# Three adaptive-modulation sums of a transformer kernel, started and reduced at other places

## The reference

```python
mod = (jax.nn.silu(c) @ w_ada[l] + b_ada[l]).reshape(b, N_SUB, 3, D_MODEL)

def sublayer(h, i, fn, resid_w):
    shift, scale, gate = mod[:, i, 0, None, :], mod[:, i, 1, None, :], mod[:, i, 2, None, :]
    u = rms_norm(h, norm_pre[l, i]) * (1.0 + scale) + shift
    return h + resid_w * gate * rms_norm(fn(u), norm_post[l, i])
```

## Time and profile before

| | us |
|---|---|
| median of 3 runs (lowest, highest) | 1827.97 (1821.05, 1828.79) |
| the profiled execution's own time | 1828.06 |
| its span | 1826.4 |
| PE busy | 1713.1 (94%) |
| DVE busy | 992.3 (54%) |
| ACT busy | 821.5 (45%) |
| POOL busy | 581.0 (32%) |

### The profile page before, as it was taken

The page is one execution under the profiler, slowest core; times in us unless marked ns, Lnnn a source line. Parts: engine busy times, 40 slices in busy tenths (PEclk is TensorE's granted clock), DMA queues, the critical chain, the costliest instruction groups (busy, mean ns, idle before and its releaser), DMA issues.

```text
span 1826.4 us, 21892 instructions
## 1 busy us (share of the span) xinstructions
PE 1713.1 (94%) x7939; PEld 1421.0 (78%) x7939; DVE 992.3 (54%) x984; ACT 821.5 (45%) x966; POOL 581.0 (32%) x378
## 2 busy tenths in 40 slices
PE   6999999999999999979879999999997987789998
PEld 5888779878888888768767888788886875678886
DVE  4445668575655565643466645654456433565444
ACT  6565541454445344424344444544445455554343
POOL 0000000188885888852888900000000010500000
PEclk9999999999999999979878999999998997789999
DMA  6656453267784778645334765546563521425552
GB/s 215 204 186 212 147 192 110 91 218 243 243 263 147 255 238 260 228 157 189 93 117 159 231 197 185 178 147 193 186 214 119 208 92 47 138 92 185 186 185 88
DMA packets 208278, 321.35 MB, mean 176 GB/s; under 512 B 10920, under 2 KB 146402, under 8 KB 208226
## 3 DMA queue, kind: packets, MB, share of 16 engines
q1 hardware_dynamic: 195968, 281.05, 47.0%
q0 software_dynamic: 10512, 38.54, 6.8%
q10 hardware_dynamic: 1746, 1.05, 0.2%
HBM read 319.55 MB, written 1.05 MB: 176 GB/s over the span
## 4 chain that ended last, share of the span: by engine, by line
PE 74%; POOL 9%; DVE 7%; ACT 5%; issue 4%; DMA 1%; ACTq 0%; POOLq 0%; SPq 0%; DVEq 0%
PE ps L544 21%; PE ps L546 21%; PE ps L545 21%; POOL arena L508 3%; POOL arena L505 3%; DVE w_lo L1606 2%; POOL arena L510 2%; PE ps L590 1%; PE ps L842 1%; ACT w_hi L1181 1%; PE ps L780 1%; PE ps L648 1%; POOL arena L512 1%; PE ps L597 1%; PE ps L947 1%
## 5 line engine op out<-in xcount | busy, mean ns | idle before, releaser
L1606 DVE TENSOR_TENSOR w_lo<-raw,w_hi 128x2048 fp32r<-128x2048 f32 x256 | 630.7, 2472 | 326.1 <-ACT w_hi L1181 325.9
L544 PE MATMUL ps<-w_hi,actT_hi 128*128 128x512 f32 x1504 | 605.6, 403 | 21.1 <-DVE actT_lo L1634 7.8
L546 PE MATMUL ps<-w_hi,actT_lo 128*128 128x512 f32 x1504 | 594.5, 395 | 0.0
L545 PE MATMUL ps<-w_lo,actT_hi 128*128 128x512 f32 x1504 | 594.4, 395 | 0.0
L1181 ACT CAST w_hi<-raw 128x2048 fp32r<-128x2048 f32 x266 | 506.1, 1911 | 192.1 <-PE ps L546 190.4
L544 PEld LDWEIGHTS ps<-w_hi,actT_hi 128*128 128x128 f32 x1504 | 288.3, 192 | 82.5 <-DVE actT_lo L1634 8.5
L546 PEld LDWEIGHTS ps<-w_hi,actT_lo 128*128 128x128 f32 x1504 | 287.5, 191 | 62.5
L545 PEld LDWEIGHTS ps<-w_lo,actT_hi 128*128 128x128 f32 x1504 | 288.5, 192 | 57.7
L544 PE MATMUL ps<-w_hi,hT_hi 128*128 128x512 f32 x480 | 188.1, 392 | 2.6 <-DVE hT_lo L1731 2.6
L545 PE MATMUL ps<-w_lo,hT_hi 128*128 128x512 f32 x480 | 187.5, 391 | 0.0
L546 PE MATMUL ps<-w_hi,hT_lo 128*128 128x512 f32 x480 | 187.5, 391 | 0.0
(11 more groups left out here) (255 smaller groups left out, 1455.4 us busy)
## 6 DMA issues: line engine op xcount, KB each, us to landing
raw<-ffn_w_in_dram SPq DMA_DIRECT2D x176, 512.0 KB, 4.8
raw<-ffn_w_out_dram SPq DMA_DIRECT2D x88, 512.0 KB, 4.4
arena<-w_ada_dram POOLq DMA_DIRECT2D x72, 512.0 KB, 5.0
raw<-ffn_w_gate_dram SPq DMA_DIRECT2D x44, 512.0 KB, 3.9
raw<-ffn_w_up_dram SPq DMA_DIRECT2D x44, 512.0 KB, 4.9
raw<-ffn_w_down_dram SPq DMA_DIRECT2D x44, 512.0 KB, 4.5
raw<-w_in_dram SPq DMA_DIRECT2D x40, 512.0 KB, 4.5
raw<-hg_w_in_dram SPq DMA_DIRECT2D x32, 512.0 KB, 4.6
```

Source lines behind the costliest of these rows:

```text
L544: nc.tensor.matmul(to, hi, whi, start=start, stop=False, skip_group_check=True)
L545: nc.tensor.matmul(to, hi, wlo, start=False, stop=False, skip_group_check=True)
L546: return nc.tensor.matmul(to, lo, whi, start=False, stop=stop, skip_group_check=True)
L1606: nc.vector.tensor_tensor(w_lo[:, s, :], raw[:, s, :], w_hi[:, s, :].bitcast(F32), ALU.subtract)\
```

## The change

POOL begins with piece 0 as soon as `silu(c)` is there, inside the first feed-forward stage, and does the `levels` copy and the zeroing behind it. Pieces 1 and 2 follow one another without a wait between them, since piece 2 is summed into a region of its own. PE reduces piece 0 behind the second chunk of hg_in, and pieces 1 and 2 between the feed-forward stage of norm 2 or 3 and the stage behind it, after the transposes of that stage's first tile. DVE's `modulation` follows in hg_in, norm 3 and norm 4. POOL's last splits of fox_in stand behind piece 2.

```diff
 HG_ORDER = (1, 0, 2, 3)
+ADA_AT = {1: 0, 3: 1, 4: 2}
...
-        ada_acc = region(12288, ADA_W)
+        ada_acc = [region(at, ADA_W) for at in (12288, 12288, 8192)]
...
-        levels_raw = region(14336, LEVEL_AT[-1])
+        levels_raw = region(10240, LEVEL_AT[-1])
...
-            pool.wait_ge(levels_loaded, 16)
-            pool.wait_ge(hT_turned, NF + 1)
-            nc.gpsimd.tensor_copy(levels, levels_raw).then_inc(levels_ready, 1)
-            pool.wait_ge(levels_ready, 1)
-            nc.gpsimd.memset(hg_sc_flat, 0.0).then_inc(hg_zeroed, 1)
-
-            pool.wait_ge(turned, 4 * (by_name["hg_out"].turned + 1))
-            pool.wait_ge(c_ready, 1)
...
-            for piece in range(3):
-                if piece:
-
-                    pool.wait_ge(ada_reduced, piece)
+            def ada_piece(piece):
                 for s in range(2):
                     ada_load(piece, s, s)
-                if piece == 2:
-                    split_gate_weights(by_name["fox_in"])
...
+            pool.wait_ge(c_ready, 1)
+            ada_piece(0)
+            pool.wait_ge(levels_loaded, 16)
+            pool.wait_ge(hT_turned, NF + 1)
+            nc.gpsimd.tensor_copy(levels, levels_raw).then_inc(levels_ready, 1)
+            pool.wait_ge(ada_reduced, 1)
+            nc.gpsimd.memset(hg_sc_flat, 0.0).then_inc(hg_zeroed, 1)
+            pool.wait_ge(turned, 4 * (by_name["hg_out"].turned + 1))
+            ada_piece(1)
+            ada_piece(2)
+            split_gate_weights(by_name["fox_in"])
             pool.wait_ge(ada_reduced, 3)
...
-                if st.norm in (3, 4, 6):
-                    ada_reduce({3: 0, 4: 1, 6: 2}[st.norm])
+                if st.norm == 1:
+                    ada_reduce(ADA_AT[st.norm])
...
                 turn_next(st, 0)
+                nxt = following[id(st)]
+                if nxt is not None and nxt.norm in (3, 4):
+                    ada_reduce(ADA_AT[nxt.norm])
...
                 chunk(st, 0, 1)
+                after_second_chunk(st)
                 chunk(st, 1, 0)
                 pe.wait_ge(kept0, st.kept + 2)
                 pe.wait_ge(kept1, st.kept + 2)
+                pe.wait_ge(mod_ready, 1)
                 turn(hg_z, 0)
...
-                pe.wait_ge(mod_ready, 2)
+                pe.wait_ge(mod_ready, 3)
...
                 weights(4)
+                act.wait_ge(levels_ready, 1)
...
                 keep(1)
+                modulation(st)
                 weights(3)
```

More of the change, by code:

```diff
@@ L511, in ada_unit @@
                 pool.wait_ge(ada_by2, n + 1)
-                nc.gpsimd.tensor_tensor(ada_acc[:, bass.ds(u * ADA_U, ADA_U)], r[:, 0, :], r[:, 1, :], ALU.add)\
+                nc.gpsimd.tensor_tensor(ada_acc[piece][:, bass.ds(u * ADA_U, ADA_U)], r[:, 0, :], r[:, 1, :], ALU.add)\
                     .then_inc(ada_summed, 1)
                 pool.wait_ge(ada_summed, n + 1)
-            for piece in range(3):
-                if piece:
-                    pool.wait_ge(ada_reduced, piece)
+            def ada_piece(piece):
                 for s in range(2):
                     ada_load(piece, s, s)
-                if piece == 2:
-                    split_gate_weights(by_name["fox_in"])
                 with pool.Fori(0, ADA_N // 2 - 1) as i:
@@ L774, in ada_reduce @@
             def ada_reduce(piece):
+                if piece == 0:
+                    pe.wait_ge(consts_loaded, 16)
                 pe.wait_ge(ada_summed, ADA_N * (piece + 1))
@@ L779, in ada_reduce @@
                 for u in range(ADA_N):
-                    last = nc.tensor.matmul(ps[:, SMALL_BANK, u:u + 1], ada_acc[:, u * P:(u + 1) * P],
+                    last = nc.tensor.matmul(ps[:, SMALL_BANK, u:u + 1], ada_acc[piece][:, u * P:(u + 1) * P],
                                             C["ones"][:, 0:1], start=True, stop=True)
@@ L1654, in modulation @@
                 n = st.norm
-                if n in (3, 4, 6):
-                    piece = {3: 0, 4: 1, 6: 2}[n]
+                if n in ADA_AT:
+                    piece = ADA_AT[n]
                     dve.wait_ge(ada_reduced, piece + 1)
```

## The result

The kernel after the change takes 1849.43 us (median of 4 runs, 1846.21 to 1850.34). The kernel before, run beside it, takes 1824.51 us (median of 4, 1818.99 to 1828.79). The ratio is 1.012, with a 95% interval of 1.0094 to 1.0145: slower, and by more than the 0.5% that a measurement of this kernel can tell. The two profiled executions have spans of 1847.7 and 1826.4 us, so the traces have 21.3 us to explain.

What follows compares the result with a forecast made beforehand. PE is busy 94%; POOL's chain counts only where PE waits for it. Terms 24.6 + 6.2 - 8.5 - 6 = +16.3 us on 1828.06 gave 1844.4 us, range 1832 to 1856.

Steps and rivals of the forecast that it cites:

- The inner range of 1836 to 1852: Whole kernel: the forecast case's time, given piece 0's end, low-clock losses, piece 2's end and the fox stage.
- Part A: Piece 0 in the first stages: PE waits for POOL in hg_in, third chunk effectively later by 24.6 us.
- I take 249: First stages: POOL's piece 0 ends at 249, nearer to the old piece 0's duration; bounds 246 to 253.
- the clock's 2.0: Behind hg_in's reduction: the low clock costs 2.0 us, between 1.4 and 2.3 in two earlier cases.
- The cover in the first stage: First stage and turn to hg_in: PE's some 9 us wait covers whatever piece 0 costs DVE and PE.
- The first rival: hg_in: piece 0 done before PE arrives, no wait, A falls to 8.5 us, time 1828 to 1831; chance 0.14.
- Part B: Pieces 1 and 2 reduced between the stages, norm 3 to fox_in: PE waits for POOL twice, +6.2 us.
- Part C: Norm 6: the reduction is taken out and gives back its price without a wait, -8.5 us.
- Part D: Fox stage: without POOL's piece 2 alongside, stretched DVE operations shorten, -6 us; bounds -12 to -2.7.
- The second: First stages: piece 0 slower than any measured, 9.6 us a unit, ending at 265, time 1860; chance 0.10.
- The third: Fox stage gives back 14 us, as DVE delays pass through exchanges between three engines; time 1836; chance 0.05.
- The fourth: The three reduction places: something other than POOL held PE, so the change might not act; no chance of its own given.

Runs made afterwards that it cites:

- the kernel with the reductions behind the chunks: Kernel after, with pieces 1 and 2 reduced behind the second chunks of norm 3 and fox_in, piece 0 still early: 1832.26 us, ratio 1.0014.
- the version with its own region: Kernel before, with only piece 1 summed into a region of its own, nothing else moved: 1817.66 us, ratio 0.9945; again 1817.15 us, ratio 0.9931.
- The third experiment: Kernel after, piece 0 reduced one chunk later in hg_in, pieces 1 and 2 behind the second chunks of norm 3 and norm 4: 1824.76 us, ratio 0.9978.

## Why the prediction was right, point by point

The predicted time was 1844.4, the measured 1849.4, and 1849.4 is within the range of 1832 to 1856. The side was right, and so was the mechanism: POOL's chain, not PE's, sets the end of three stretches. Against the profiled execution the sum was +16.3 and the traces have +21.3. The terms were off by +2.9, -1.4, +0.6, 0, +6.5 and -3.6, in the order of the table; that they sum to no more than 5.0 is in part luck. The inner range of 1836 to 1852 was narrower than its own bounds, which give 1831 to 1856 when they all fall on one side. Term by term:

**Part A, predicted +24.6, measured +27.5.** Piece 0 ended at 250.93, where I had taken 249 with bounds of 246 to 253: its 216.1 us are those of the old piece 0 (216.2), where I had drawn the value in a little for quicker last units. POOL started at 34.9, and its first unit was late, ending 17 us behind the start, since the first product waited for its load until 41.68 and then ran stretched. The later units were quicker, so the whole came out even. PE arrived at 241.0 and waited 10.1 us, not at 240 for 9. The reduction took 10.4 as predicted. The clock behind it stayed low for longer than assumed, at 0.55 in the mean for 6.7 us, and cost 2.9 us in place of 2.0: the third chunk took 13.8 us, where 48 products at 0.227 us each take 10.9. These rows are the reduction and the stretch behind it:

```profile
251.00:261.00 10.00, 9.92 (x47) 9.95 (x47) 0.00 (x0) 0.00 (x0) 0.66 (x1) 0.50 0.01 2
261.30:268.00 6.70, 6.70 (x18) 5.28 (x19) 4.92 (x5) 0.00 (x0) 1.80 (x1) 0.55 0.39 122
```

The steps that were short are "I take 249", by 1.9 us and inside its bounds, and the clock's 2.0, which came out above its upper bound of 2.3. The HGRN2 stage took 1.4 us less, which I had put at nothing, and in these two profiles only: the stretch varies by 3 to 5 us within each kernel, as shown above.

**The cover in the first stage** held. DVE's splits in norm 0 went from 2292 ns to this:

```profile
L1612 DVE TENSOR_TENSOR w_lo<-raw,w_hi 128x2048 fp32r<-128x2048 f32 x30 | 83.4, 2779 | 49.1 <-ACT w_hi L1186 49.1
```

2779 ns is what they take in norm 2 beside POOL, 2796. The feed-forward stage was no longer for it, +0.3 us. But the turn to hg_in was: PE's first product of hg_in waited 4.42 us for the rounded activations (2.03 before), and DVE's operation that scales them ahead of the transposes, 0.75 us before, took 3.05:

```profile
215.03 0.79 PE L542 MATMUL ps<-w_hi,actT_hi 128*128 128x512 f32 x1 [4.42 <-DVE actT_lo L1627]
...
206.42 3.05 DVE L1646 TENSOR_SCALAR arena<-x,small 128x1024 f32<-128x1024 f32 x1
```

Since PE had then to wait for POOL anyway, this cost nothing in the end. It also hangs on how the operations of the two engines happen to fall. After's second profile has it as well (3.04 us), but in the five other kernels with the same work up to here the operation took 0.83 to 0.87 us and PE's first product of hg_in waited 2.04. In after POOL began a product at 206.99, while the operation ran (206.42 to 209.47); in the kernel with the reductions behind the chunks it ran from 205.69 to 206.52, when POOL was ending a unit, and the next product began at 207.65:

```profile
205.69 0.83 DVE L1643 TENSOR_SCALAR arena<-x,small 128x1024 f32<-128x1024 f32 x1
```

DVE and POOL do slow each other in the mean: a split went from 2292 to 2779 ns, and POOL's units behind the late first one took 8.65 us each, against the 6.4 of the fox stage where DVE has little to do. The Trainium skill, "SBUF — State Buffer", section "Who interferes with whom", calls the port pair that the two share an exclusive lock, and the trace agrees in so far as both engines took longer side by side. The first rival (piece 0 done before PE arrives, 24 units in 202 us) fell with it.

**Part B, predicted +6.2, measured +6.8.** The waits were 11.2 and 9.2 where I had 8.9 and 11.7: piece 1 took 218.8 us and not 216.2, piece 2 209.2 and not 212.5. So the first wait was too short in my sum and the second too long, and most of the two errors cancelled: the term came within 0.6 us partly by this luck. Both reductions took 10.4. (A second profile of after has 11.63 and 9.21, so the two waits are steady. The wait at fox_in of the kernel before is not: 10.7, 15.0 and 10.5 us in its three profiles.)

**Part C, predicted -8.5, measured -8.5.** The transposes of norm 6 are 16.81 us apart, as those of norm 8:

```profile
1234.23 0.60 PE L646 MATMUL ps<-consts_sb,hidden 128*128 128x128 f32 x4
1251.04 0.60 PE L646 MATMUL ps<-consts_sb,hidden 128*128 128x128 f32 x4
```

**Part D, predicted -6, measured +0.5 between the two executions and -4 in the mean of all.** This is the term that was mis-sized most. The DVE operations did get shorter, as said: L1941 takes 4.50 us for two where it took 7.28, L1965 at the same place in the stage 0.17 where it took 1.64, and the split 2.29 where it took 3.82. (The other three of before's L1958 took 0.17 to 0.21, so that one was hit once in four times.)

```profile
917.71 4.50 DVE L1941 TENSOR_TENSOR arena<-arena,small 128x2048 f32<-128x2048 f32 x2
...
963.77 0.17 DVE L1965 TENSOR_SCALAR small<-small 128x8 f32<-128x8 f32 x1
...
991.68 2.29 DVE L1612 TENSOR_TENSOR w_lo<-raw,w_hi 128x2048 fp32r<-128x2048 f32 x1
```

After's L1963, the same operation as before's L1956, starts 27.7 us late the first time, 934.48 against 906.83, down from 32.9: 5.2 gained. The third time it is 34.9 late, 962.52 against 927.65. In between lie these windows of PE, two of before and two of after, over about the same work (columns as in the earlier trace rows):

```profile
912.00:922.00 10.00, 8.11 (x48) 7.12 (x46) 5.14 (x7) 7.88 (x34) 7.58 (x9) 0.83 0.17 53
922.00:932.00 10.00, 5.78 (x44) 5.28 (x42) 6.74 (x8) 3.57 (x9) 8.77 (x9) 0.84 0.35 105
...
947.00:957.00 10.00, 9.57 (x36) 8.48 (x36) 1.57 (x4) 5.88 (x18) 0.00 (x0) 0.50 0.01 2
957.00:967.00 10.00, 8.49 (x37) 7.81 (x37) 6.83 (x10) 3.61 (x15) 0.00 (x0) 0.50 0.00 1
```

Before had a granted clock of 0.83 there and after 0.50, and the gain went back; that the clock took it is inferred from this pair of profiles, not shown. The error in this term is to have read the stage from a single execution as if its length were fixed. Before's had been the shortest of its three.

**Later, predicted nothing, measured -3.6.** This is luck of the same kind: before's first profile has the longest token mixer of its three, 230.7 us against 224.4 and 227.4. Over the whole program it cancels 3.6 of the 6.5 us by which the fox stage was off, which is why a sum with a wrong D comes within 5 us of the span.

**The rivals.** The second (9.6 us a unit) missed: the units took 9.0 in the mean, start-up loads or not. The third would have needed 14 us in the fox stage. The fourth fell with the three waits.

What I had not weighed is why the reduction stands where it does. The third experiment shows that the same early pieces, reduced one place later, lose nothing against the kernel before that could be measured; and the version with its own region shows that the useful part of the change is its smallest one.

## What to carry to other kernels

Where a helper engine runs a chain beside the main one, work out two clocks, when the chain ends and when the main engine gets there, and put the meeting point behind both: a wait of 10 us costs more than 10 us if the clock is low behind it, as it was here. Before moving work earlier, look whether the chain has an idle stretch that only a shared buffer causes (17.5 us here), for here a second region took it out and gave some 10 us. A gain of a few us in one stage should be read from several executions, since here the same kernel's stage moved by 4 us and more from one to the next.

## What the runs showed of the hardware

The granted clock fell during or right behind the reductions, a stream of one-column float32 products, although PE was busy throughout: to 0.56 within the one of norm 6 in before, and to 0.71 in the 5.8 us behind the shortest of all, which had itself run at 1.00. When PE came to a reduction with no wait ahead, the 48 instructions took between 5.4 and 8.0 us over all kernels; behind a wait of 5 us or more they took 10.4 each time, at 0.50. I had taken 6.2 as the fixed price. The length follows the mean clock: their product is 5.2 to 5.4 us. The fall behind a reduction belongs to its price too, and in norm 6 of before the two made up the same 8.5 us in three profiles. What decides when the clock falls stays open.

The clock in the fox stage is not the same from one execution to the next of one kernel, 0.76, 0.73 and 0.70 in three of the kernel before, with stage times of 121.5 to 126.0 us. The code and the order of the work on each engine are the same. The cause stays open.
